# Long convolution of a two-block network: the last chunk's stacking copies on two queues, seven products left out

## The reference, cut to what matters

```
h = x @ pw1_w + pw1_b                      # 1024 -> 2048
a, g = split(h);  h = a * sigmoid(g)       # 512 x 1024
h = causal_dwconv(h, dw_w, dw_b)           # 31 taps, each channel by itself
h = layer_norm(h);  h = silu(h)
return h @ pw2_w + pw2_b
```

## Time and profile before

| | |
|---|---|
| time, median of 3 runs | 1946.94 us (1946.56 to 1947.49) |
| time of the profiled execution | 1947.36 us |
| its span, first to last instruction | 1945.6 us |
| PE busy | 1898.1 us, 98% of the span |
| DVE, ACT, POOL busy | 1060.8, 749.7 and 179.6 us |
| mean granted clock of TensorE | 0.995 of full speed |

### The profile page before, as it was taken

The page is one execution under the profiler, slowest core; times in us unless marked ns, Lnnn a source line. Parts: engine busy times, 40 slices in busy tenths (PEclk is TensorE's granted clock), DMA queues, the critical chain, the costliest instruction groups (busy, mean ns, idle before and its releaser), DMA issues.

```text
span 1945.6 us, 23088 instructions
## 1 busy us (share of the span) xinstructions
PE 1898.1 (98%) x9211; PEld 1528.3 (79%) x9211; DVE 1060.8 (55%) x1278; ACT 749.7 (39%) x993; POOL 179.6 (9%) x124
## 2 busy tenths in 40 slices
PE   6999999999999998999999999999999999999997
PEld 4767788877788765888888888888778888888886
DVE  6874442256435878845555533542686645555434
ACT  5533342244323546542222222543673523232223
POOL 5600000000000445110000000200000200000001
PEclk9999999999999999999999999999999999999998
DMA  9211222211132444122323233222102222323321
GB/s 400 88 66 60 82 98 99 96 66 44 66 108 87 132 133 142 65 87 88 106 88 106 87 110 107 87 87 87 44 1 98 79 94 86 108 86 104 112 90 62
DMA packets 31053, 186.46 MB, mean 96 GB/s; under 512 B 3329, under 2 KB 5505, under 8 KB 10498
## 3 DMA queue, kind: packets, MB, share of 16 engines
q1 hardware_dynamic: 29392, 175.96, 26.7%
q10 hardware_dynamic: 1586, 9.44, 1.2%
HBM read 174.64 MB, written 2.10 MB: 91 GB/s over the span
## 4 chain that ended last, share of the span: by engine, by line
PE 94%; DVE 2%; ACT 2%; issue 1%; POOL 1%; DMA 0%; ACTq 0%; SPq 0%; POOLq 0%; DVEq 0%
PE PS L599 26%; PE PS L601 26%; PE PS L600 26%; PE PS L1156 2%; PE PS L667 1%; PE PS L669 1%; PE PS L668 1%; PE PS L1037 1%; PE PS L961 1%; PE PS L1168 1%; PE PS L980 1%; PE PS L1127 1%; PE PS L1130 1%; PE PS L924 1%; ACT WH L1203 0%
## 5 line engine op out<-in xcount | busy, mean ns | idle before, releaser
L599 PE MATMUL PS<-H,WH 128*128 128x512 f32 (+1 forms) x1616 | 624.3, 386 | 15.6 <-POOL L L497 7.4
L601 PE MATMUL PS<-H,WL 128*128 128x512 f32 (+1 forms) x1616 | 617.8, 382 | 0.0
L600 PE MATMUL PS<-L,WH 128*128 128x512 f32 (+1 forms) x1616 | 617.6, 382 | 0.0
L1777 DVE TENSOR_TENSOR WL<-RAW,WH 128x2048 fp32r<-128x2048 f32 x134 | 311.3, 2323 | 267.7 <-ACT WH L1203 263.3
L599 PEld LDWEIGHTS PS<-H,WH 128*128 128x128 f32 x1616 | 305.7, 189 | 86.3 <-issue 10.3
L1203 ACT ACTIVATE WH<-RAW 128x2048 fp32r<-128x2048 f32 x141 | 269.0, 1909 | 221.4 <-PE PS L601 183.0
L601 PEld LDWEIGHTS PS<-H,WL 128*128 128x128 f32 x1616 | 305.4, 189 | 59.4
L600 PEld LDWEIGHTS PS<-L,WH 128*128 128x128 f32 x1616 | 305.6, 189 | 56.3 <-issue 0.2
L460 POOL TENSOR_TENSOR L<-X,H 128x512 fp32r<-128x512 f32 x32 | 48.9, 1538 | 1261.7 <-ACT H L1581 720.8
L1649 ACT ACTIVATE TT<-TT 128x512 f32<-128x512 f32 x44 | 27.8, 632 | 310.4 <-DVE TT L2470 310.4
L599 PE MATMUL PS<-FH,WH 128*128 128x512 f32 (+1 forms) x376 | 142.8, 380 | 0.0
(11 more groups left out here) (365 smaller groups left out, 2494.6 us busy)
## 6 DMA issues: line engine op xcount, KB each, us to landing
RAW<-w SPq DMA_DIRECT2D x148, 1024.0 KB, 4.9
HS<-HC SPq DMA_DIRECT2D x32, 264.0 KB, 4.9
ADA<-w_ada ACTq DMA_DIRECT2D x4, 1024.0 KB, 23.6
ADA<-w_ada SPq DMA_DIRECT2D x4, 1024.0 KB, 23.0
GA<-w_gate SPq DMA_DIRECT2D x1, 4096.0 KB, 19.9
PWR<-w_ple ACTq DMA_DIRECT2D x2, 1024.0 KB, 4.9
out<-X SPq DMA_DIRECT2D x8, 256.0 KB, 2.1
X<-x_t SPq DMA_DIRECT2D x2, 512.0 KB, 6.5
```

Of the source, the lines that this page charges most:

```text
L599: nc.tensor.matmul(ps, wh, xh, start=start, stop=False, skip_group_check=skip)
L600: nc.tensor.matmul(ps, wh, xl, start=False, stop=False, skip_group_check=skip)
L601: return nc.tensor.matmul(ps, wl, xh, start=False, stop=stop, skip_group_check=skip)
L1777: v.tensor_tensor(WL[:, p], RAW[:, p], WH[:, p].bitcast(F32), ALU.subtract).then_inc(w_lo, 1)
```

## The change

The four stacking copies of the last chunk are divided: SP issues g = 0 and 1 as before, ACT issues g = 2 and 3, right behind the last sigmoid and with the same two waits that SP has. The other chunks keep their four copies on SP. The seven matmuls of `idle` ahead of the last chunk's taps are taken out; the function stays, for its other use in the attention.

```diff
+        def four_shifts(m, g):
+            rows_g = HC[32 * g:32 * g + 32, m, 0:HSW]
+            return bass.AP(rows_g.tensor, rows_g.offset, [list(rows_g.ap[0]), [1, TAPS], [1, HSW]])
...
                 sp.wait_ge(bank_free, GROUP0["pw1"] + m + 1)
                 if m >= 3:
                     sp.wait_ge(cp_ps, m - 2)
-                for g in range(4):
-                    rows_g = HC[32 * g:32 * g + 32, m, 0:HSW]
-                    shifted = bass.AP(rows_g.tensor, rows_g.offset, [list(rows_g.ap[0]), [1, TAPS], [1, HSW]])
-                    sp.dma_start(HS[:, m % 3, g, :], shifted).then_inc(hs_in[m % 3], 16)
+                for g in range(4 if m < KC - 1 else 2):
+                    sp.dma_start(HS[:, m % 3, g, :], four_shifts(m, g)).then_inc(hs_in[m % 3], 16)
...
                 if m == KC - 1:
                     pe.wait_ge(cm_done, 1)
-                    idle(PS[:, 7, :], H[:, 0, :], 7)
                 pe.wait_ge(hs_in[m % 3], 16 * TAPS * (m // 3 + 1))
...
                 if m == KC - 1:
+                    act.wait_ge(bank_free, GROUP0["pw1"] + KC)
+                    act.wait_ge(cp_ps, m - 2)
+                    for g in (2, 3):
+                        act.dma_start(HS[:, m % 3, g, :], four_shifts(m, g)).then_inc(hs_in[m % 3], 16)
                     whole_square(KC - 3)
                     whole_square(KC - 2)
```

## The result

The changed kernel takes 1950.62 us (median of 22 runs, 1948.48 to 1952.06), the kernel before in the same comparison 1947.28 us (22 runs, 1946.11 to 1950.06). The ratio is 1.0015, with a 95% interval of 1.0009 to 1.0021: 0.15% slower, 3.3 us by the medians, and 1 (no change) lies outside the interval. The forecast was 1945.5 us, with a range up to 1947.5.

A forecast was written before the change was run, and what follows sets the result against it. PE was taken to bound the kernel, busy for 98% of the span. The profiled 1947.36 us less a 1.48 us gain gave 1945.9; with the median 0.42 lower, 1945.5 us was forecast, range 1944.2 to 1947.5.

The forecast's parts named there:

- PE idles 3.07 us for nothing, the landing ends it.: Ahead of the last chunk's taps: 3.07 us without useful PE work, ended by the fourth copy's landing; the most to gain.
- The copies on two queues.: Last chunk's copies: the fourth issued at 741.3 instead of 743.38, landing after 5.72 us at 747.0 instead of 749.1.
- The weight load beside them: SP's 1 MB load leaves at about 741.9 instead of 745.56, beside ACT's copies; half a microsecond in the range.
- 3.07 us need not either: PE's pause before the last taps: the clock stayed up 4.2 us in another pause, so no fall here; cost 0.
- the seven products, put at 0: Matmuls of `idle` before the last taps: removal alone gives nothing, 1.90 us under the landing, and costs no clock; 0.
- The second rival.: Weight load gets ahead of ACT's copies: landing 752.1, clock falls, 7.5 us slower, 1954.4; chance 0.07, 0.03 with clock falling.
- What is late next.: After the last taps: once copies land earlier, POOL's, DVE's and ACT's unmoved work limits the gain to 1.48 us.
- The bound on ACT: After ACT's table load, ending 752.98, two load issues, then squares at 753.92; the last statistics come 1.48 us earlier.
- The issues cost nothing on ACT.: ACT's two copy issues end before chunk 5's squares can run at 744.69, even if they take 4 us; cost 0.
- The start of `pw2`.: First 96 matmuls of the next stage: the clock's rise moves along, end 1.48 us earlier; range 0.85 to 1.7 us.
- the case of the rise that stays where it is: Start of `pw2`: the clock still rises at 768.5, so the stage ends at 777.1, only 0.85 us earlier.
- The range.: Whole kernel: 1944.2 us (1.7 us gain and half a microsecond of spread) to 1947.5 us (no gain, same spread).

The follow-up runs named there:

- e5: The changed kernel with 22 matmuls of `idle` ahead of the last chunk's taps instead of none; 1950.31 us, ratio to the kernel before 1.0014.
- e8: e1_hold with the seven matmuls of `idle` put back ahead of the last taps; 1946.67 us, ratio to the kernel before 0.9994.
- e1_hold: The changed kernel, with SP holding the 1 MB weight load until the last chunk's four copies have landed; 1946.54 us, ratio to the kernel before 0.9994.
- e3: The kernel before without its seven matmuls of `idle`, all four copies on SP; 1948.14 us, ratio to the kernel before 1.0001.
- e2: The changed kernel with the seven matmuls of `idle` back ahead of the last taps; 1950.43 us, ratio to the kernel before 1.0017.
- e7: e1_hold with the copies paired otherwise, g = 0 and 2 on SP, 1 and 3 on ACT; 1945.86 us, ratio to the kernel before 0.9993.

## Why the prediction was wrong, by its steps

- **PE idles 3.07 us for nothing, the landing ends it.** Right; the end moved with the landing in every version but e5 and e8, where the products end later than the copies land.
- **The copies on two queues.** The step itself was nearly right: 747.0 was taken, and with the load out of the way the last copy landed at 747.48, 6.14 us after its issue where 5.72 was taken. What came off is mainly issue time: the last issue is at 741.34 and not at 743.38, and the time to landing grew by 0.4.
- **The weight load beside them: "half a microsecond in my range".** This is the step that failed. The load was seen to leave SP 3.7 us earlier (3.2 in the trace), and the harm was priced at 0.5 us because nobody waits for the load. It was 3.4 us in the time to landing (9.54 against 6.14). The argument against the rival was that the load stands third on SP's queue, "behind as many copies as ACT's queue has". But ACT's queue was slower: its copies landed 5.6 and 9.5 us after issue, SP's 4.5 and 6.1. From 747.5 on SP's queue held only the load, and ACT's last copy was still on its way. Without this step the next one would not have counted: in e1_hold the pause is 1.51 us and the clock stays up.
- **"3.07 us need not either" (the clock).** The second step that failed, a term put at 0 that was 2.05 us of slower taps in the changed kernel. One row showed a clock still up 4.2 us into a pause, and from it a limit was read that other pauses would have to pass. The changed kernel's clock fell 2.3 us into its pause, that of e3 2.2 us into one of 2.68 us, that of e2 behind a pause of 2.90 us; in e7 it stayed up over a pause of 2.45 us. And that row was one execution: in the same place, the 7.5 us ahead of `pw2`, the clock of e1_hold fell only 2.8 us in. PE's last matmul ends at 755.75 there, and this window has 0.50 for its last 0.2 us:

```profile
757.00:758.75 1.75, 0.00 (x0) 0.00 (x0) 1.57 (x4) 1.10 (x4) 0.00 (x0) 0.95 0.78 257
```

  Over the ten traces the fall came 2.7 to 4.8 us into that pause, with the program there the same. For the seven products, put at 0, the trace of e3 shows 1.4 us of slower taps.
- **The second rival.** Its mechanism came true and its price was too high: 7.5 us against 3.97. The landing came at 751.0 and not at 752.1. The load cost it 3.5 us, somewhat more than the 3.0 taken, but counted from the 747.5 of e1_hold: the rival had set the gain of the two queues at nothing and counted from 749.1. And the clock came back at about 755.3, within the taps, so they took 6.55 us and not 9.0. The start of the taps from which it was to decide, 750.4, rested on the same reading of the clock. It had a chance of 0.07, of which 0.03 with the clock falling.
- **What is late next.** The landing decided in e1 after all: L1056's counterpart starts at 752.04, right behind the taps, 0.2 us after POOL's last sum. The bound on ACT was not one. The stretch of e1_hold is shorter by 1.48 us, the very number that I had worked out from that bound; this is luck. The rows of ACT in e1_hold:

```profile
751.66 1.28 ACT L1557 ACT_TABLE_LOAD   x1
752.17 0.35 ACTq L1504 DMA_DIRECT2D PWR<-w_ple  x1
752.55 0.45 ACTq L1505 DMA_DIRECT2D PR<-p_t  x1
753.10 0.72 ACT L1563 ACTIVATE SQV<-CV 128x256 f32<-128x256 f32 x2 [0.16 <-DVE CV L2280]
```

  The two issues run while the table still loads, so the squares start at 753.10 and not 753.9.
- **The issues cost nothing on ACT.** Right: they last 2.49 us, and the squares of chunk 5 start 0.1 us later than before, as all else does.
- **The start of `pw2`.** In e1_hold 96 products take from 763.25 to 777.28, 14.03 us instead of 13.22: of the 1.52 us by which they start earlier, 0.71 are left. That is the case of the rise that stays where it is (0.85 was its price). But it is one execution, with the early fall shown above: e8, with nearly the same stretch (24.46 against 24.22 us), takes 13.40 us there, e7 13.03, the changed kernel 13.16. What this step gives or takes changes from one execution to the next by up to 1 us, and the prediction, which read its price from one trace, could not have known it.
- **The range.** Its lower end is a slip: 1946.94 less 1.7 and less 0.5 is 1944.7, not 1944.2. It decides nothing here, since the result lies above the upper end.

The Trainium skill's rule that was set against the change ("DMA: Bandwidth & Descriptors", section "Issuing engines are not separate DMA queues") says that DMAs from several engines interleave on the same 16 DMA engines and that two issuers save only issue time. These traces agree with both halves. The saved issue time is the gain of e1_hold: the last copy is issued 2.0 us earlier, with one issue of 0.67 us ahead of it and not three of 0.55, 0.60 and 1.43 us, and lands 1.6 us earlier. The interleaving is the loss of the changed kernel.

## What to carry to other kernels

When transfers are spread over two queues, look at what each queue issues next: the queue that is relieved starts its next bulk load earlier, beside the other queue's copies. Keep the transfer that is waited for ahead of that load on the same queue, or hold the load until the copies have landed; both took the loss away here, though neither is shown to beat the kernel before. One row of a pause that the clock survived is no limit for another pause, nor for the same pause in another execution; price an unfilled pause ahead of short work with the clock down.

## What the runs showed that I had not expected

- One and the same 264 KB copy took 9.54 us to land beside a 1 MB load on the other queue (9.5 in two more traces), 6.14 us without it (6.2 in one more). The same load behind the copies on one queue changed nothing (5.70 against 5.72 us).
- TensorE's clock fell from 2.4 to 1.2 GHz 2.2 and 2.3 us into pauses of PE (e3, changed kernel) and once just after a pause of 2.90 us (e2). In the pause ahead of `pw2`, the same in all ten kernels, it fell 2.7 us in (e5) at the earliest and 4.8 us in (e8) at the latest.
- ACT issues DMAs while its activation table loads: at 752.17 within a load from 751.66 to 752.94.
- In one execution, copies that read neighbouring groups of 32 partitions at the same time had their last landing 0.94 us later than the same copies in another pairing (7.08 against 6.14 us after the last issue).
